# Second tile of the attention's output gate: 16 float32 products from unsplit weights and input among the chunk steps, not among the dense products

## What is computed

```python
proj = h @ p['w_in_ab'][j]
pr, pg = proj[..., :RWKV_PROJ], proj[..., RWKV_PROJ:]
...
q, kg, vg, gz, og = jnp.split(pg.astype(f32), list(GLA_SPLITS), axis=-1)
...
o_g = rms_norm(o_g, p['gla_norm_w'][j]).reshape(bsz, t_len, GLA_VDIM) * jax.nn.silu(og)
out = jnp.concatenate([o_rwkv, o_g], axis=-1).astype(h.dtype) @ p['w_out_ab'][j]
```

## Time and profile before

| what | value |
|---|---|
| median of 3 runs | 1468.73 us (1468.45 to 1468.87) |
| the profiled execution's own time | 1469.37 us |
| its span, first to last instruction | 1467.7 us |
| PE busy | 1428.1 us (97%) |
| DVE busy | 1173.1 us (80%) |
| ACT busy | 950.7 us (65%) |
| mean granted TensorE clock | 0.995 of full speed |

### The profile page before, as it was taken

One profiled execution on the slowest core, in us unless ns is written; L12 is line 12 of the kernel. 1 busy time (PEld: TensorE's weight loads), 2 busy tenths in 40 slices (PEclk: granted clock), 3 DMA queues, 4 the chain that ended last, 5 costly groups with the idle time before them and its releaser, 6 DMA issues.

```text
span 1467.7 us, 29198 instructions
## 1 busy us (share of the span) xinstructions
PE 1428.1 (97%) x11253; PEld 1278.1 (87%) x11254; DVE 1173.1 (80%) x1580; ACT 950.7 (65%) x1257; POOL 76.3 (5%) x152
## 2 busy tenths in 40 slices
PE   7999989999999999999999999999999999999997
PEld 7999988999999899888788888888888888888884
DVE  5686579545535789867998998899988999898997
ACT  4465455433323696476778787778777887877873
POOL 8300000000000000000000000000000000000000
PEclk9999999999999999999999999999999999999999
DMA  8431004544445262217999999999999999999992
GB/s 261 152 106 37 2 15 145 173 144 145 150 143 164 88 187 88 88 59 285 339 390 397 402 394 398 347 396 380 371 397 350 407 379 362 397 353 410 390 345 93
DMA packets 162214, 371.62 MB, mean 253 GB/s; under 512 B 10232, under 2 KB 85968, under 8 KB 162128
## 3 DMA queue, kind: packets, MB, share of 16 engines
q1 hardware_dynamic: 159352, 361.18, 67.2%
q0 software_dynamic: 2160, 7.87, 2.0%
q10 hardware_dynamic: 616, 1.37, 0.2%
HBM read 360.68 MB, written 9.71 MB: 252 GB/s over the span
## 4 chain that ended last, share of the span: by engine, by line
PE 88%; DVE 7%; ACT 3%; issue 1%; DMA 1%; SPq 0%; DVEq 0%; ACTq 0%
PE psum L1371 11%; PE psum L1372 11%; PE psum L1373 11%; PE psum L596 10%; PE psum L598 9%; PE psum L597 9%; PE psum L1395 5%; PE psum L1397 5%; PE psum L1396 5%; PE psum L712 2%; PE psum L1380 1%; PE psum L696 1%; PE psum L1133 1%; DVE wd_lo L1468 1%; PE psum L609 1%
## 5 line engine op out<-in xcount | busy, mean ns | idle before, releaser
L2184 DVE TENSOR_TENSOR w_lo<-moe_ring,w_hi 128x1024 fp32r<-128x1024 f32 (+1 forms) x560 | 608.3, 1155 | 28.9 <-ACT w_hi L2916 28.9
L2916 ACT ACTIVATE w_hi<-moe_ring 128x1024 fp32r<-128x1024 f32 (+1 forms) x560 | 531.6, 1015 | 69.4 <-PE psum L1397 39.0
L1371 PE MATMUL psum<-w_hi,xe_hi 128*128 128x512 f32 (+1 forms) x768 | 288.1, 375 | 1.6 <-DVE w_lo L2184 1.4
L1372 PE MATMUL psum<-w_hi,xe_lo 128*128 128x512 f32 (+1 forms) x768 | 285.9, 372 | 0.0
L1373 PE MATMUL psum<-w_lo,xe_hi 128*128 128x512 f32 (+1 forms) x768 | 285.4, 372 | 0.0
L1468 DVE TENSOR_TENSOR wd_lo<-arena,wd_hi 128x1024 fp32r<-128x1024 f32 x141 | 169.9, 1208 | 132.9 <-ACT wd_hi L2441 132.6
L596 PE MATMUL psum<-in_hi,wd_hi 128*128 128x320 f32 x800 | 250.5, 313 | 2.5 <-DVE wd_lo L1468 1.2
L2441 ACT ACTIVATE wd_hi<-arena 128x1024 fp32r<-128x1024 f32 (+1 forms) x140 | 146.2, 1047 | 157.4 <-PE psum L598 151.8
L598 PE MATMUL psum<-in_hi,wd_lo 128*128 128x320 f32 x800 | 247.2, 309 | 0.0
L597 PE MATMUL psum<-in_lo,wd_hi 128*128 128x320 f32 x800 | 247.1, 309 | 0.0
L1371 PEld LDWEIGHTS psum<-w_hi,xe_hi 128*128 128x128 f32 x768 | 144.5, 188 | 28.4 <-DVE w_lo L2184 2.9
(11 more groups left out here) (449 smaller groups left out, 1799.5 us busy)
## 6 DMA issues: line engine op xcount, KB each, us to landing
moe_ring<-in_moe_w SPq DMA_DIRECT2D x216, 1024.0 KB, 8.8
moe_ring<-in_moe_w SPq DMA_DIRECT2D x64, 768.0 KB, 5.7
arena<-in_ffn_w SPq DMA_DIRECT2D x30, 1024.0 KB, 5.3
arena<-in_w_in_c SPq DMA_DIRECT2D x16, 1024.0 KB, 5.5
arena<-in_w_in_ab SPq DMA_DIRECT2D x12, 1024.0 KB, 5.5
arena<-in_w_out_ab SPq DMA_DIRECT2D x4, 1024.0 KB, 5.1
arena<-in_w_out_c SPq DMA_DIRECT2D x4, 1024.0 KB, 5.0
arena<-in_ffn_w SPq DMA_DIRECT2D x4, 768.0 KB, 4.3
```

The lines of the kernel that those rows point to most:

```text
L1371: pe.matmul(b[:, 0:w], xe_hi[:, k, :], hi_[:, c0:c1], start=(k == 0), stop=False)
L1372: pe.matmul(b[:, 0:w], xe_lo[:, k, :], hi_[:, c0:c1], start=False, stop=False)
L2184: dve.tensor_tensor(w_lo[:, i % UNITS, 0:unit_words(i)], moe_unit(i), w_hi[:, i % UNITS, 0:unit_words(i)], ALU.subtract)\
L2916: act.activation(w_hi[:, i % UNITS, 0:unit_words(i)], moe_unit(i), ACT.Copy).then_inc(S("e_hi"), 1)
```

## The change

Tile 12 is no longer split. Its 2 x 8 products are made as float32 matmuls straight from the tile in the ring and from the unsplit input `xT`, in PSUM bank 0, two, one or none at each of three places of each chunk step (`GATE_STEPS`). As the function Silu is not in the table that is loaded then, the gate's two blocks are made from Abs, Exp and Ln on ACT and two operations on DVE: x * exp(min(x, 0) - ln(1 + exp(-|x|))). The counters skip the two halves of tile 12, and SP loads tile 16 into the ring's place of tile 12 only when its products are done.

The core of the diff:

```diff
                 if h == 0:
-                    mm.then_inc(S("dense_half"), 1)
+                    mm.then_inc(S("dense_half"), 2 if i == GATE_T - 1 else 1)
...
-            dense_pair(AB_T + 12, 0, "ab", 24, "ab_full", "ab_done")
+            turn[0] += 2
+            gate_at = [0]
+
+            def gate_products(n):
+
+                for _ in range(n):
+                    j, k = divmod(gate_at[0], KC)
+                    gate_at[0] += 1
+                    if j == k == 0:
+                        pe.wait_ge(*at_count(f"tile_in{GATE_T % DENSE_RING}", 16 * (GATE_T // DENSE_RING + 1)))
+                    if k == 0:
+                        take(("ab", 2 * GATE_T + j), "ab_done", 2 * GATE_T + j + 1, score_at)
+                    mm = pe.matmul(where["ab", 2 * GATE_T + j][:, 0:T], tile_of(GATE_T)[:, k, j * P:(j + 1) * P], xT[:, k, :],
+                                   start=k == 0, stop=k == KC - 1)
+                    if k == KC - 1:
+                        mm.then_inc(S("ab_full"), 1)
...
+            GATE_STEPS = [(0, 2, 2), (2, 1, 1), (2, 1, 2), (1, 2, 0)]
...
+                gate_products(GATE_STEPS[i][0])
                 pe.wait_ge(*at_count("w1_done", i + 1))
...
+                gate_products(GATE_STEPS[i][1])
                 pe.wait_ge(*at_count("u_done", i + 1))
...
                     .then_inc(S("seq_full"), 1)
+                gate_products(GATE_STEPS[i][2])
             gla_updates()
```

On DVE, `half_rest` of tile 12's halves goes (the last of tile 11 counts for three), and four short operations come:

```diff
-            half_rest(2 * (AB_T + 12))
...
-                if f == 2:
-                    half_rest(2 * (AB_T + 12) + 1)
...
+            def gate_shifted(j):
+
+                e, x = gla["E"][:, j, :], gog[:, 2 + j, :]
+                dve.wait_ge(*at_count("gate_logs", j + 1))
+                dve.scalar_tensor_tensor(e, x, 0.0, e, ALU.min, ALU.subtract).then_inc(S("gate_shifted"), 1)
+
+            def gate_opened(j):
+
+                x = gog[:, 2 + j, :]
+                dve.wait_ge(*at_count("gate_sigmoid", j + 1))
+                dve.tensor_tensor(x, x, gla["E"][:, j, :], ALU.mult).then_inc(S("gate_opened"), 1)
...
+                elif i == 2:
+                    gate_shifted(0)
                 elif i == 3:
...
                     norm_squares(0, NEARLY, 0)
+                    gate_opened(0)
...
             gla_state(4)
+            gate_shifted(1)
```

`gate_opened(1)` stands at the head of `attention_end`. On ACT, the rounding of tile 12 and `projected(12)` go, and these come, `gate_logs(0)` behind the o copy of step 1, `gate_sigmoid(0)` behind that of step 2, `gate_logs(1)` behind the second norm and ahead of a `half_rounded`, `gate_sigmoid(1)` in `attention_end`:

```diff
-            dense_rounded(AB_T + 12)
...
-            projected(12)
...
+            def gate_logs(j):
+
+                e, x = gla["E"][:, j, :], gog[:, 2 + j, :]
+                act.wait_ge(*at_count("ab_full", 2 * GATE_T + j + 1))
+                act.wait_ge(*at_count("gla_qk", 2))
+                act.activation(x, where["ab", 2 * GATE_T + j][:, 0:T], ACT.Copy).then_inc(S("ab_done"), 1)
+                act.wait_ge(*at_count("ab_done", 2 * GATE_T + j + 1))
+                link(act.activation(e, x, ACT.Abs))
+                link(act.activation(e, e, ACT.Exp, scale=-1.0))
+                act.activation(e, e, ACT.Ln, bias=1.0).then_inc(S("gate_logs"), 1)
...
             norm_std(NEARLY, NCH, 1)
+            gate_logs(1)
             half_rounded(2 * (OUT_T + 1))
```

On SP:

```diff
-            for i in range(OUT_T, OUT_T + 4):
+            for i in range(OUT_T, OUT_T + 3):
                 load_tile(i)
...
+            sp.wait_ge(*at_count("ab_full", 2 * OUT_T))
+            load_tile(OUT_T + 3)
             sp.wait_ge(*at_count("hout_done", 1))
```

More of the change, by code:

```diff
@@ L487, in mixed_trunk @@
         AB_T, OUT_T = 0, len(AB_COLS)
+        GATE_T = OUT_T - 1
         FFN_T = OUT_T + D // SC
@@ L1462, in link, with half_rest @@
                 dve.wait_ge(S("dve_chain"), chain[0])
-            def half_rest(m_):
+            def half_rest(m_, units=1):
                 dve.wait_ge(*at_count("dense_hi", m_ + 1))
@@ L1468, in half_rest @@
                 dve.tensor_tensor(wd_lo[:, m_ % DENSE_UNITS, 0:words], src, rounded_of(m_)[:, 0:words],
-                                  ALU.subtract).then_inc(S("dense_lo"), 1)
+                                  ALU.subtract).then_inc(S("dense_lo"), units)
             def dense_rest(i):
@@ L1549, in _ @@
             dve.tensor_tensor(PRC[:, :, 0, :], s2, kkT, ALU.mult).then_inc(S("bonus_in"), 1)
-            half_rest(2 * (AB_T + 11) + 1)
+            half_rest(2 * (AB_T + 11) + 1, 3)
             dve.tensor_tensor(PRC[:, :, 1, :], s1, XS[:, 0:4, :], ALU.mult)
-            half_rest(2 * (AB_T + 12))
             dve.tensor_copy(dC[:, :, :], s1.rearrange("p f (c t) -> p f c t", c=NCH)[:, :, :, C - 1])
@@ L1665, in attention_end @@
                 n_, NH = a["name"], a["heads"]
+                gate_opened(1)
+                dve.wait_ge(*at_count("gate_opened", 2))
                 dve.wait_ge(*at_count(n_ + "_o", 4))
@@ L2429, in logs_and_exps, with half_rounded @@
                 act.preload_act_table_set("natural_log_exp_and_others")
-            def half_rounded(m_):
+            def half_rounded(m_, units=1):
                 i = m_ // 2
@@ L2440, in half_rounded @@
                 src, words = half_of(m_)
-                act.activation(rounded_of(m_)[:, 0:words], src, ACT.Copy).then_inc(S("dense_hi"), 1)
+                act.activation(rounded_of(m_)[:, 0:words], src, ACT.Copy).then_inc(S("dense_hi"), units)
             def dense_rounded(i):
@@ L2522, in _ @@
             act.activation(QT, QT, ACT.Exp, scale=-0.5).then_inc(S("decay_exp"), 1)
-            dense_rounded(AB_T + 11)
+            half_rounded(2 * (AB_T + 11))
+            half_rounded(2 * (AB_T + 11) + 1, 3)
             projected(10)
-            dense_rounded(AB_T + 12)
             projected(11)
@@ L2602, in attention_end @@
                 rounded(1)
+                gate_sigmoid(1)
                 act.wait_ge(*at_count(n_ + "_o", 4))
@@ L2652, in norm_std, with gate_sigmoid @@
                 act.activation(stat[:, 1, cols], stat[:, 1, cols], ACT.Exp, scale=-0.5).then_inc(S("gn_std"), 1)
+            def gate_logs(j):
[7 more added lines that the diff above has]
+                act.activation(e, e, ACT.Ln, bias=1.0).then_inc(S("gate_logs"), 1)
+            def gate_sigmoid(j):
+                e = gla["E"][:, j, :]
+                act.wait_ge(*at_count("gate_shifted", j + 1))
+                act.activation(e, e, ACT.Exp).then_inc(S("gate_sigmoid"), 1)
             NEARLY = PLACE[STEPS[1][-1]] + 1
@@ L2667, in _ @@
                    .then_inc(S("o_done"), 1)
+                if i == 1:
+                    gate_logs(0)
+                elif i == 2:
+                    gate_sigmoid(0)
             act.wait_ge(*at_count("gla_ds_full", 1))
```

## The result

The changed kernel takes 1473.07 us, the median of 15 runs (1469.82 to 1477.29); before, 1468.48 in 15 runs (1467.13 to 1470.67). The ratio is 1.0037 with a 95% interval from 1.0029 to 1.0044: slower by about 5 us, above the predicted range of 1465.6 to 1471.9. By the forecast's own marks (over 1471.7 is slower) this is the case that had a chance of 0.17. The profiled execution took 1474.83 us, with a span of 1473.1 and a mean granted clock of 0.993.

What follows compares the result with a forecast made beforehand. PE, busy 97% of the span, was taken as the bound, with ACT's queue behind tile 12 also on the path. Front -5.8, steps +4.6 and bank 0 +1.7 summed to +0.5 us: 1469.2 us forecast, range 1465.6 to 1471.9.

Steps and rivals of the forecast that it cites:

- the case that had a chance of 0.17: Whole kernel: a measured time over 1471.7 us, counted as slower; chance 0.17.
- Front, -5.8: Up to DVE's mask: without tile 12's split, ACT's table load starts earlier and PE goes on 5.8 us sooner (5.0 to 6.5).
- Bank 0, +1.7: Behind the steps: PE waits 1.7 us (1.0 to 2.2) until ACT releases bank 0 for GLA's output.
- Steps, +4.6: Chunk steps: 16 float32 products, partly hidden in PE's waits, lengthen them by 4.6 us (2.3 to 6.3).
- The changes between large and small matmuls: Chunk steps on PE: each switch costs up to 0.1 us more, nine blocks, 0.9 us.
- What hides: Chunk steps: of 8.6 us of products, PE's free places cover all but 3.7 us, before switches are added.
- modelled tail: PE's waits in the chunk steps: about 0.2 us, the last small matmul's tail, added to each idle time as free place.
- a product is 0.54 us: Chunk steps on PE: each float32 product takes 0.54 us, read from the norm's matmuls; sixteen take 8.6 us.
- ACT's copy keeps 0.70 us: ACT in step 2: the gate's first-block operations, 1.9 us, hide ahead of the copy of u with 0.7 us to spare.
- the load of tile 16 is hidden: SP's DMA starts about 190 us with idle queues and is needed near 220 us; cost 0.
- the granted clock falls: Rival: behind the 1.8 us wait at the mask the clock halves for 6.8 us, costing 3.4, total 1472.6 us; chance 0.07.

Runs made afterwards that it cites:

- E2: Against the changed kernel, ACT copies the gate's last block out of bank 0 earlier, right behind step 3's copy and ahead of the norm; 1470.34 us, ratio 1.0016.
- E7: Against the changed kernel, all 16 float32 products stand in a row behind the gz products, ahead of the scores, none in the steps; 1471.52 us, ratio 1.0022.
- E12: The changed kernel unedited, its fourth profile, one run; 1478.06 us, span 1476.3 us.
- E3: Against the changed kernel, 12 of the 16 float32 products left out (gate values wrong), wait at bank 0 kept; 1470.31 us, ratio 1.0013.
- E1: The changed kernel again, unedited, for a second profile and more times; 1474.78 us in 6 runs, ratio 1.0046.
- E11: The changed kernel unedited, its third profile, one run; 1470.04 us, span 1468.3 us.
- E5: Against the changed kernel, the 16 products stand as four blocks of four, one at each step's end, bank 0's wait kept; 1471.64 us, ratio 1.0031.
- E4: Against the changed kernel, seven spare 128 x 128 transposes added on PE in the wait at bank 0; 1471.88 us, ratio 1.0024.
- E6: Against the changed kernel, four products at each step's end and ACT's copy out of bank 0 made earlier; 1469.04 us, ratio 1.0008.
- E8: Against the changed kernel, eight products behind gz, two at each step's end, and ACT's copy out of bank 0 made earlier; 1468.91 us, ratio 1.0011.

## Why the prediction was wrong

**Front, -5.8: right.** -5.7 in all four profiles. The row for the table load was the one to go by.

**Bank 0, +1.7: right.** +1.7 in the profiles, and E2 removes it exactly.

**Steps, +4.6: the step that failed.** They grew by 7.3. Its parts:
- *The changes between large and small matmuls.* I put "up to 0.1" on each of nine blocks, 0.9 in all, without a row for it. There are ten blocks, six of 1.27 or 1.28 us and four of 0.73 to 0.81: 10.7 us, against 8.6 for sixteen times 0.54, and 8.8 in a row (E7). A block costs about 0.2 us beyond its products, 2.1 in all: 1.2 too little. The price of a block of two stood in the trace of before: between small matmuls, from 119.91 to 121.18, 1.27 us. I had taken the product's price from L830, where four stand in a row among the dense ones.

```profile
119.91 1.34 PE L725 MATMUL psum<-gz_s,gate_up 128*128 128x320 f32 x4
121.18 1.85 PE L856 MATMUL psum<-arena 64*64 64x128 f32 x30
```

- *What hides.* Of 9.5 us of work (8.6 and 0.9) I had 4.6 left over and so 4.9 hidden; 10.7 less 7.3 is 3.4: 1.5 too much. About 1.0 of it is step 0. There I took a place of 0.39 us as free in which PE waited for nothing that the trace shows ("issue"). After the change such a pause stands at 170.41 [0.56] ahead of the block, beside the products and not under them (0.56 to 0.83 in all four profiles). The rest is the "modelled tail" of 0.2 us that I added to each free place. The rows of the steps showed 4.2 us of idle time before (0.39, 0.85, 0.75, 0.75, 0.39, 1.03) and show 1.4 after (0.56, 0.84). These 2.8 us are most of what hid; of the tails, 1.2 us in my sum, at most 0.6 came.

Step 0 on PE before the change, from the last scores to the next step's head:

```profile
176.29 1.28 PE L761 MATMUL psum<-arena 64*64 64x32 f32 x38
...
180.38 0.27 PE L712 MATMUL psum<-arena 64*64 64x64 f32 x1 [0.39 <-issue]
...
182.85 1.36 PE L712 MATMUL psum<-arena 64*64 64x64 f32 x52 [0.85 <-DVE arena L1785]
```

and the same two marks in the changed kernel:

```profile
167.79 1.28 PE L778 MATMUL psum<-arena 64*64 64x32 f32 x38
...
176.28 0.93 PE L729 MATMUL psum<-arena 64*64 64x64 f32 x48
```

That is 6.56 us before and 8.49 after, 1.9 more, where the forecast had 0.5 and two blocks' 0.2. Steps 1, 2 and 3 grew by 1.6, 2.2 and 1.5 between these two profiles, where the forecast had 1.4, 1.5 and 1.1 with the blocks' 0.1; their heads are full, as planned. In the means of all profiles the steps alone grew by 7.6 us (19.3 to 26.9 from L761's start to the updates); 0.3 came back in the stretch between mask and steps.

The forecast's other steps hold: a product is 0.54 us, ACT's copy keeps 0.70 us, and the load of tile 16 is hidden (between 170 and 260 us no engine waits on a DMA).

**The sum's second gap: what the steps don't show.** +3.3 of work on 1468.5 is 1471.8, just inside the range's end. By its ratio the kernel is 5.4 us slower (4.3 to 6.5). The rest are stretches that differ between executions of the same program: a fall of the clock behind the bank's wait in two of four profiles (1.1 us from output to projection in one, 2.7 in the other, and 0.3 more behind it), and a longer end in three of four (1.1 to 2.1 us). None of the three profiles of before has either. The longer wait at the first expert product (1.4 us in two of four, one of three before) may add to it. The forecast had no term for any of these. The rival "the granted clock falls" named the wrong wait: it put the fall behind the 1.67 us at the mask, behind which the clock stayed full in every profile, and priced it at 3.4 with a chance of 0.07. I had written that 1.03 us at 195.80 left the clock full, and did not ask the same of the 1.7 us that my own sum adds just behind it.

**What stays open.** The wait at bank 0 and the fall belong together, as counts over all executions show. In the 14 profiles the mean granted clock of the whole execution is 0.993 or lower just where the fall stands behind the steps (the first, E12, E3), and 0.995 or higher in the other eleven. By that mark the fall came as follows:

| versions | wait at bank 0 | executions at 0.993 or lower |
|---|---|---|
| changed kernel (first result, E1, E11, E12) | 1.6 us idle | 10 of 23 |
| E3 | 1.6 us idle | 9 of 12 |
| E5 | 1.6 us idle | 3 of 8 |
| E4 | filled, 0.7 us idle | 0 of 8 |
| E2, E6, E7, E8 | none | 2 of 12, 1 of 12, 0 of 8, 1 of 11 |
| the kernel before, beside E1 to E8 | none | 0 of 55 |

That is 22 of 43 with the wait and 4 of 51 without it or with it filled. The mark is not exact, since other low stretches move the mean as well. What decides in a single execution stays open, and so does part of the time: the time beyond the work (ratio less 1, times 1468, less the growth of the work up to the projection) is 2.1 us for the changed kernel, 2.2 for E5 and 3.9 for E3 (all with the wait), 0.3 for E4 (filled), 0.9, 1.0 and -0.4 for E2, E6 and E7 (no wait), but 1.9 for E8, which has no wait either; each has an interval of 1 us or more. Nor is it settled what lets the two instruction fetches meet at the end.

## What to carry to other kernels

Work put into another stage's gaps costs its switches too: count blocks, not only matmuls, and take their price from a row where such a block stands among the same neighbours. Count a gap as free only where the engine waits for another engine, not where the profile says "issue", and add no tail to it. Where the sum itself creates a wait on TensorE, ask at that place too whether the clock can fall behind it, and what the median would be then. One profile of each kernel can't tell work from the execution's luck: here profiles of one program spread over 8.0 us, while three stretches between marks repeated within 0.6.

## What the runs showed of the hardware

- Whether the clock falls differs between executions of one program: behind the steps not at all in E1 and E11, for some 7 us in the first profile and some 10 in E12. By the mean granted clock it fell in about half of the executions with 1.6 us of idle time there, and in 4 of 51 without it. The 1.67 us at the mask were followed by no fall in any profile.
- A single float32 product of 128 x 128 by 320 among 64 x 64 matmuls holds PE for 0.73 us, two for 1.28, sixteen in a row for 8.81: about 0.2 us for each block, however long.
- A product whose input was ready started 0.65 to 1.04 us late at the program's end in the five of 14 profiles in which two instruction fetches of 16 KB stood 0.3 to 0.8 us apart ahead of it. That one caused the other was not tested.
